# Narrow weight columns loaded from ScalarE's queue; the opening, the convolution block and the end reordered; three fillers per router left out

## The chip, the core and the metric

One core of a Trainium2 chip runs one launch of the whole program. The metric is the device time of that launch in microseconds (us), lower is better.

## The reference

The program is two transformer blocks on one sequence of 256 tokens of width 1024, all in float32. The first has two layers. In each, `x @ w_in` makes inputs of a gated linear attention and of a spatial gating unit; their outputs go through `w_out`, a residual and a layer norm, then through cross attention to 256 memory tokens with another residual and norm, then through 16 experts:

```python
scores = softmax(xt @ w_router + b_router)             # 16 affinities per token
g_sel  = argmax(sum of the top 2 in each of 4 groups)  # one group, two experts in it
y      = sum_e gate[:, e] * ((silu(xt @ w_gate[e]) * (xt @ w_up[e])) @ w_down[e])
x      = layer_norm(alpha * x + y)
```

The second block has an attention of 8 heads beside a state space mixer, whose input `xbc` passes a causal convolution of four taps and a SiLU, then `w_out_a`, `w_out_b`, `w_out`, 16 more experts, and at the end

```python
x = x + sigmoid(x @ w_ple_gate) * (p @ w_ple_proj)
return rms_norm(x, final_norm_g)
```

## The kernel before, in words

**Precision.** A float32 product is made of three products of a faster type: a weight unit (128 x 1024) and each activation are split in a high part and a low part. ScalarE writes the high part (`split`, L1470), VectorE the low part (`split`, L1829) behind it, and TensorE multiplies high by high, high by low and low by high. A dense product of 512 columns takes four units. Six units fit in `w_high`, so ScalarE's `split` of unit n waits until TensorE is done with unit n - 6, and a few splits that stand ahead of a read-out in ScalarE's program tie it to TensorE.

**Engines.** Each engine has its own program, in an order written out by hand, and waits on semaphores. SyncE issues the stream of weight loads, 387 of 1 MB (L595), into nine buffers and, in the expert stages, into other tiles that are free then ("lent"). GpSimd issues the small loads and takes square roots (`root`, L655). PSUM is four slots of two banks. A planner (`plan_job`, `plan_dense`, `between`) hands slots out in the order of TensorE's program; `begin` waits until a slot's last user has freed it.

**The opening.** SyncE loads the two tiles of x (L588), then weights. TensorE transposes both (L912), ScalarE and VectorE split them (L1484, L1849), then the first units, and the product `qk` begins (L749, L750, L754): with `head`, the high products of two units for tile 0, then tile 1, then the low ones. GpSimd waits for two weight loads and then issues six loads of narrow columns (L633): two of the low rank gate, the router, dt, and two of the second router. Each of five of them has 1024 runs of 64 bytes. ScalarE waits for all six (L1628) behind nine splits; VectorE makes the low part (L2201); TensorE then makes `aT` from 16 columns (L931).

**The router** (`router`, `places`, `experts`). Per token tile TensorE transposes, runs fillers (products of constants into an unused bank, L940), multiplies by the router's columns (L954) with one more filler before the fifth of eight, and adds the residual (L1004), with one filler behind it. VectorE ranks and picks; TensorE counts places (L1174, L1176) and gathers each expert's tokens (L996), which ScalarE copies (`packed`, L1539) after it has waited for the gates and written them into `turner` (L1520). In the second block the gates need an `Exp` in between (L1787). Then 16 experts run, each gate, up (L1079) and down (L1114). `FILLERS` (16 in layer 1, two records each) run behind the last expert of a layer while the norm is computed (`norm_of_sums`, `finished`).

**The convolution block.** TensorE makes `xb0`, `xb1`, `xb2`, `z0`, `z1` with attention steps in between (`values_mixed`, `weights_turned` L1334, `scores`). VectorE convolves a block (L2335, L2337). ScalarE reads out, then runs `conv_silu` (L1707, four instructions) of the block before, then `mixed_high` (L1478), whose result VectorE splits and so frees the slot that the next block needs. Behind `z1` `sources` needs all three blocks' SiLU (L1371). Then four gate products follow, each with a scan (`scanned`, L1398 to L1401) and the next scan's decays (`decays`, L1386) behind it.

**The end.** Behind the last expert TensorE multiplies `p` by `w_ple_proj` (`pp`, two units, L799), then transposes x (L912), whose high and low parts it needs for `w_ple_gate` (`pg`, eight units).

The lines that set the order at the router and at the end:

```python
filler(2 * job[name][0] + 1, 1)                   # in router, ahead of the fifth product
filler(2 * job[name][0] + 1, 1)                   # in places, behind the residual
dense_rows(("2.pp0", "2.pp1"), 1, (p_high, p_low))
turn_tiles(x, ("2.x2T0", "2.x2T1"), S["moe_added"])
```

Of the kernel before, what the change touches and what calls it, by code (L numbers as in the profile page):

```python
# [20 lines left out]
ACT = mybir.ActivationFunctionType  # L21
# [3 lines left out]
P = 128  # L25
# [3 lines left out]
SPLIT = 6  # L29
# [4 lines left out]
FILLERS = (8, 16, 0)  # L34
# [17 lines left out]
def build(nc, a, out):  # L52
# [132 lines left out]
    for l in range(DEPTH):  # L185
# [17 lines left out]
        for b, q_slots in enumerate(((s1, s3), (s0, s2))):  # L203
# [15 lines left out]
               "z0": ("oT2", "pT3", "cs"), "z1": ("oT3", "csT", "cb", "xs0", "xs1"), "ga0": ("csb0",), "ga1": ("y0", "csb1"),  # L219
               "gb0": ("y1", "csb2"), "gb1": ("y2", "csb3")}  # L220
# [10 lines left out]
    products, turns_in = slots_of("2.ya0", "2.ya1"), slots_of("2.csb3", "2.y3")  # L231
# [48 lines left out]
    with ExitStack() as ctx:  # L280
# [305 lines left out]
        def _(sp):  # L586
            for t in range(TT):
                sp.dma_start(x[:, t, :], a["x"][0, t * P:t * P + P, :]).then_inc(x_loaded[t], 16)  # L588
            for n, (src, m) in enumerate(stream):
                if raw_behind[n] >= 0:  # L590
                    wait_emptied(sp, raw_behind[n])
# [11 lines left out]
        def _(pool):  # L603
# [22 lines left out]
            with nc.allow_non_contiguous_dma(reason="narrow weight columns, loaded once"):  # L626
                for i in range(2):
                    pool.wait_ge(loaded[i], 16)
                for w, k0, k, dst in ([(a["w_in"][l], O_A, RANK, nar_cols(nar_raw, N_A[l], RANK)) for l in range(DEPTH)]
                                      + [(a["w_router"], 0, NE, router_w[:, :, 0:NE]), (a["w_in_2"][0], O_DT2, SH, nar_cols(nar_raw, N_DT, SH)),  # L630
                                         (a["w_re_2"][0], 0, NE, router_w[:, :, NE:2 * NE]), (a["w_rg_2"][0], 0, 4, router_w[:, :, 2 * NE:2 * NE + 4])]):
                    src = w.rearrange("(c p) n -> p c n", p=P)[:, :, k0:k0 + k]
                    pool.dma_start(dst, src).then_inc(S["narrow_loaded"], 16)  # L633
# [71 lines left out]
        def _(pe):  # L705
# [236 lines left out]
            def router(name, names, m, c0, width, src, normed_before):  # L942

                for t in range(TT):
# [5 lines left out]
                    for c in range(KC):  # L950
                        if c == KC // 2:
                            filler(2 * job[name][0] + 1, 1)
                            pe.wait_ge(S["back_turned"], TT * m + t + 1)
# [212 lines left out]
            def places(name, m):  # L1166

                begin(name)
                filler(2 * job[name][0] + 1, 1)
# [15 lines left out]
            for l in range(DEPTH):  # L1185
                L = f"{l}."

                if l == 0:
                    for t in range(TT):
                        pe.wait_ge(x_loaded[t], 16)  # L1190
                        turn_tiles(x[:, t:t + 1, :], (L + f"xT{t}",))
                else:
# [1335 lines left out]
```

## Time and profile before

| | us |
|---|---|
| median of 3 runs (lowest, highest) | 1446.82 (1443.25, 1447.17) |
| the profiled execution | 1447.49 |
| its span | 1445.8 |
| TensorE busy | 1383.8 (96%) |
| VectorE busy | 596.8 (41%) |
| ScalarE busy | 490.4 (34%) |
| granted TensorE clock, mean | 0.983 |
| DMA, mean over the span | 292 GB/s |

### The profile page before, as it was taken

To read this page: it belongs to the slowest core of one execution; us is meant where nothing else is said; L and a number is where in the kernel's file an instruction comes from. 1 tells how busy PE (TensorE), PEld (TensorE's weight loads), DVE (VectorE), ACT (ScalarE), POOL (GpSimd) and SP (SyncE) were. 2 spreads that over 40 slices of the span, in tenths; PEclk is the share of its full clock that TensorE was granted. 3 is DMA by queue.
4 is the path that set the end of the run, shared out by engine and by line. 5 is a ranking of instruction groups with operands and counts; after the bars stand their busy time and mean duration, and the time that the engine had idled before them with its cause. 6 is when DMAs were issued, how large, how long until landed. Compare 5 with 4: busy or idle time off the path is not lost.

```text
span 1445.8 us, 21087 instructions
## 1 busy us (share of the span) xinstructions
PE 1383.8 (96%) x8985; PEld 1008.7 (70%) x8985; DVE 596.8 (41%) x1004; ACT 490.4 (34%) x692; POOL 55.6 (4%) x95
## 2 busy tenths in 40 slices
PE   5999999999998999999999999899999999999996
PEld 4788977655654788987655554788787776565555
DVE  4586535111114585645211111657766661111125
ACT  4554444111113644443211111466564431111123
POOL 5000000000001000000000000100000000000000
PEclk8999999999999999999999999999998999999998
DMA  9646458999999655628999999753443559999990
GB/s 329 236 147 202 147 199 322 421 420 421 422 420 400 238 171 176 204 87 337 373 420 421 421 420 412 258 174 118 135 157 117 226 235 422 420 421 421 420 373 30
DMA packets 90803, 422.64 MB, mean 292 GB/s; under 512 B 7068, under 2 KB 7232, under 8 KB 53840
## 3 DMA queue, kind: packets, MB, share of 16 engines
q1 hardware_dynamic: 86528, 407.92, 72.2%
q0 software_dynamic: 4176, 13.30, 2.6%
q8 instruction: 74, 1.21, 0.3%
q14 instruction: 25, 0.20, 0.0%
HBM read 420.15 MB, written 1.05 MB: 291 GB/s over the span
## 4 chain that ended last, share of the span: by engine, by line
PE 89%; DVE 4%; ACT 3%; issue 2%; DMA 1%; POOL 1%; SPq 0%; DVEq 0%; POOLq 0%; ACTq 0%
PE ps L1079 23%; PE ps L1114 11%; PE ps L749 5%; PE ps L754 5%; PE ps L750 5%; PE ps L799 4%; PE ps L865 4%; PE ps L804 4%; PE ps L800 4%; PE ps L1126 4%; PE ps L872 4%; PE ps L866 4%; PE ps L996 3%; PE ps L912 1%; PE ps L1093 1%
## 5 line engine op out<-in xcount | busy, mean ns | idle before, releaser
L1829 DVE TENSOR_TENSOR raw_low<-raw,w_high 128x1024 fp32r<-128x1024 f32 x198 | 237.9, 1222 | 167.1 <-ACT w_high L1470 166.5
L1470 ACT ACTIVATE w_high<-raw 128x1024 fp32r<-128x1024 f32 x198 | 206.7, 1057 | 253.6 <-PE ps L754 110.8
L1577 ACT ACTIVATE out_high<-ps,stats 128x512 fp32r<-128x512 f32 x48 | 33.0, 687 | 305.2 <-PE ps L1114 305.2
L749 PE MATMUL ps<-w_high,act_high 128*128 128x512 f32 x272 | 109.8, 404 | 8.4 <-DVE raw_low L1829 3.6
L2154 DVE TENSOR_TENSOR hid<-silu_g,ps 128x256 f32<-128x256 f32 x48 | 29.3, 611 | 210.2 <-PE ps L1079 210.2
L1114 PE MATMUL ps<-raw,hT 128*64 128x512 f32 x488 | 110.3, 592 | 0.0
L750 PE MATMUL ps<-raw_low,act_high 128*128 128x512 f32 x272 | 107.7, 396 | 0.0
L2163 DVE SCALAR_TENSOR_TENSOR out_low<-ps,stats,out_high 128x512 fp32r<-128x512 f32 x48 | 36.1, 752 | 167.6 <-ACT out_high L1577 167.6
L754 PE MATMUL ps<-w_high,act_low 128*128 128x512 f32 x272 | 104.7, 393 | 0.0
L865 PE MATMUL ps<-act_high,w_high 128*128 128x256 f32 x288 | 82.6, 289 | 5.7 <-issue 3.4
L866 PE MATMUL ps<-act_high,raw_low 128*128 128x256 f32 x288 | 82.1, 287 | 0.0
L1079 PE MATMUL ps<-raw,own_odd 128*64 128x256 f32 x704 | 81.5, 381 | 0.0
L872 PE MATMUL ps<-act_low,w_high 128*128 128x256 f32 x288 | 80.2, 287 | 0.0
L799 PE MATMUL ps<-w_high,act_high 128*128 128x512 f32 x192 | 76.3, 398 | 4.0 <-DVE act_low L1849 4.0
L2159 DVE COPY hT<-ps 128x256 f32<-128x256 f32 x45 | 19.1, 425 | 147.4 <-PE ps L1093 147.4
L800 PE MATMUL ps<-raw_low,act_high 128*128 128x512 f32 x192 | 75.7, 394 | 0.0
L1114 PEld LDWEIGHTS ps<-raw,hT 128*64 128x64 f32 x488 | 34.9, 137 | 56.6 <-issue 52.1
L1079 PE MATMUL ps<-raw,own_even 128*64 128x256 f32 x624 | 72.2, 381 | 0.0
L1079 PEld LDWEIGHTS ps<-raw,own_odd 128*64 128x64 f32 x704 | 49.4, 137 | 31.3 <-issue 9.2
L749 PEld LDWEIGHTS ps<-w_high,act_high 128*128 128x128 f32 x272 | 52.2, 192 | 23.1 <-issue 7.8
L655 POOL TENSOR_TENSOR stats<-stats,exponent 128x1 f32<-128x1 f32 (+2 forms) x24 | 21.8, 910 | 1183.8 <-DVE stats L1898 287.1
L1568 ACT ACTIVATE silu_g<-ps 128x256 f32<-128x256 f32 x48 | 18.5, 385 | 139.7 <-PE ps L1079 139.7
(417 smaller groups left out, 2546.2 us busy)
## 6 DMA issues: line engine op xcount, KB each, us to landing
raw<-in_w_down SPq DMA_DIRECT2D x64, 1024.0 KB, 20.4
raw<-in_w_in SPq DMA_DIRECT2D x44, 1024.0 KB, 14.1
raw<-in_w_up SPq DMA_DIRECT2D x43, 1024.0 KB, 15.1
raw<-in_w_gate SPq DMA_DIRECT2D x40, 1024.0 KB, 19.4
work<-in_w_gate SPq DMA_DIRECT2D x26, 1024.0 KB, 16.4
w_lent<-in_w_gate SPq DMA_DIRECT2D x25, 1024.0 KB, 18.9
work<-in_w_up SPq DMA_DIRECT2D x19, 1024.0 KB, 19.2
w_lent<-in_w_up SPq DMA_DIRECT2D x16, 1024.0 KB, 15.0
```

The costliest lines, as they stand in the source:

```text
L749: pe.matmul(bank[:, t, :], xh, wh, start=(k == 0), stop=False)
L750: pe.matmul(bank[:, t, :], xh, wl, start=False, stop=False)
L754: return pe.matmul(bank[:, t, :], src[1][:, k, t * P:t * P + P], weights(n, 512 * c, 512 * c + 512)[0], start=False, stop=(k == KC - 1))
L799: pe.matmul(slot_banks(names[t])[:, b, :], xh, wh, start=(k == 0), stop=False)
L800: pe.matmul(slot_banks(names[t])[:, b, :], xh, wl, start=False, stop=False)
L865: pe.matmul(bank, wh, src[0][:, k, 0:T], start=(k == 0), stop=False)
L866: pe.matmul(bank, wl, src[0][:, k, 0:T], start=False, stop=False)
L872: return pe.matmul(bank, wh, src[1][:, k, 0:T], start=False, stop=(k == KC - 1))
L1079: i = pe.matmul((G, U)[part][OWN * h:OWN * h + OWN, 0:256], own[e // QUAD % 2][:, c, OWN * (e % QUAD):OWN * (e % QUAD) + OWN], w[:, FF * r ...
L1114: i = pe.matmul(y[OWN * h:OWN * h + OWN, :], turned[:, r, OWN * j:OWN * j + OWN], w[:, D * r + 512 * h:D * r + 512 * h + 512], start=(j + ...
L1470: A(split_unit(n)[0], raw_unit(n), ACT.Copy).then_inc(high_ready, 1)
L1829: V.tensor_tensor(split_unit(n)[1], raw_unit(n), split_unit(n)[0].bitcast(F32), ALU.subtract).then_inc(low_ready, 1)
```

## The change

The six narrow loads leave GpSimd's queue for ScalarE's, behind the third unit's split; GpSimd goes on to the small loads of layer 0 at once. The second tile of x is loaded behind the first weights; its transposes go between the high products of the two tiles, and the first two splits go ahead of it. The filler inside each router's products and the one behind the residual go. ScalarE packs before it waits for the gates. At the end of layer 1 a split on VectorE moves behind both scalings, and four more fillers run. The three `conv_silu` move behind `z1`'s splits. The decays go into the middle of the next product, ahead of the scan. At the end, x is transposed before `pp` is made.

```diff
@@ -31,7 +31,7 @@
 TAIL = 3
-FILLERS = (8, 16, 0)
+FILLERS = (8, 20, 0)
 SLOTS = 4
@@ -216,8 +216,8 @@
     between = {"q": ("dtT", "dt"), "v": ("s0",), "xb0": ("pT0", "s1"), "xb1": ("oT0", "pT1", "s2"), "xb2": ("oT1", "pT2", "s3"),
-               "z0": ("oT2", "pT3", "cs"), "z1": ("oT3", "csT", "cb", "xs0", "xs1"), "ga0": ("csb0",), "ga1": ("y0", "csb1"),
-               "gb0": ("y1", "csb2"), "gb1": ("y2", "csb3")}
+               "z0": ("oT2", "pT3", "cs"), "z1": ("oT3", "csT", "cb", "xs0", "xs1"), "ga0": ("csb0",), "ga1": ("csb1", "y0"),
+               "gb0": ("csb2", "y1"), "gb1": ("csb3", "y2")}
     for name, c0 in columns.items():
@@ -228,7 +228,7 @@
     plan_job("2.y3")
-    products, turns_in = slots_of("2.ya0", "2.ya1"), slots_of("2.csb3", "2.y3")
+    products, turns_in = slots_of("2.ya0", "2.ya1"), slots_of("2.y2", "2.y3")
     plan_in(turns_in, "2.uT0", "2.uT1")
@@ -584,9 +584,10 @@
         def _(sp):
-            for t in range(TT):
-                sp.dma_start(x[:, t, :], a["x"][0, t * P:t * P + P, :]).then_inc(x_loaded[t], 16)
+            sp.dma_start(x[:, 0, :], a["x"][0, 0:P, :]).then_inc(x_loaded[0], 16)
             for n, (src, m) in enumerate(stream):
+                if n == 1:
+                    sp.dma_start(x[:, 1, :], a["x"][0, P:2 * P, :]).then_inc(x_loaded[1], 16)
                 if raw_behind[n] >= 0:
@@ -623,14 +624,8 @@
             nc.gpsimd.memset(st[:], 0.0).then_inc(S["consts_ready"], 1)
-            with nc.allow_non_contiguous_dma(reason="narrow weight columns, loaded once"):
-                for i in range(2):
-                    pool.wait_ge(loaded[i], 16)
-                for w, k0, k, dst in ([(a["w_in"][l], O_A, RANK, nar_cols(nar_raw, N_A[l], RANK)) for l in range(DEPTH)]
-                                      + [(a["w_router"], 0, NE, router_w[:, :, 0:NE]), (a["w_in_2"][0], O_DT2, SH, nar_cols(nar_raw, N_DT, SH)),
-                                         (a["w_re_2"][0], 0, NE, router_w[:, :, NE:2 * NE]), (a["w_rg_2"][0], 0, 4, router_w[:, :, 2 * NE:2 * NE + 4])]):
-                    src = w.rearrange("(c p) n -> p c n", p=P)[:, :, k0:k0 + k]
-                    pool.dma_start(dst, src).then_inc(S["narrow_loaded"], 16)
+            for i in range(2):
+                pool.wait_ge(loaded[i], 16)
             def load_small():
@@ -949,7 +944,6 @@
                         if c == KC // 2:
-                            filler(2 * job[name][0] + 1, 1)
                             pe.wait_ge(S["back_turned"], TT * m + t + 1)
@@ -1166,7 +1160,6 @@
                 begin(name)
-                filler(2 * job[name][0] + 1, 1)
                 pe.wait_ge(S["picks_ready"], m + 1)
@@ -1185,14 +1178,9 @@
 
-                if l == 0:
-                    for t in range(TT):
-                        pe.wait_ge(x_loaded[t], 16)
-                        turn_tiles(x[:, t:t + 1, :], (L + f"xT{t}",))
-                else:
-                    turn_tiles(x[:, 0:1, :], (L + "xT0",), S["normed"], TT * (3 * l - 1))
-                second = (lambda: turn_tiles(x[:, 1:2, :], (L + "xT1",), S["normed"], TT * (3 * l - 1) + 1)) if l else None
-                dense_cols(L + "qk", head=(L + "xT0", L + "xT1"), between=second)
+                x_is_in = [(x_loaded[t], 15) if l == 0 else (S["normed"], TT * (3 * l - 1) + t) for t in range(TT)]
+                turn_tiles(x[:, 0:1, :], (L + "xT0",), *x_is_in[0])
+                dense_cols(L + "qk", head=(L + "xT0", L + "xT1"), between=lambda: turn_tiles(x[:, 1:2, :], (L + "xT1",), *x_is_in[1]))
                 if l == 0:
@@ -1427,9 +1415,8 @@
             for k, name in enumerate(("2.ga1", "2.gb0", "2.gb1")):
-                dense_cols(name)
+                dense_cols(name, after_two=lambda: decays(k + 1))
                 scanned(k)
-                decays(k + 1)
             operand_ready(*[f"2.oT{k}" for k in range(AH // 2)])
@@ -1442,8 +1429,8 @@
             operand_ready("2.pT")
+            turn_tiles(x, ("2.x2T0", "2.x2T1"), S["moe_added"])
             dense_rows(("2.pp0", "2.pp1"), 1, (p_high, p_low))
-            turn_tiles(x, ("2.x2T0", "2.x2T1"), S["moe_added"])
             operand_ready("2.x2T0", "2.x2T1")
@@ -1470,6 +1457,15 @@
 
+            def load_narrow():
+
+                with nc.allow_non_contiguous_dma(reason="narrow weight columns, loaded once"):
+                    for w, k0, k, dst in ([(a["w_in"][l], O_A, RANK, nar_cols(nar_raw, N_A[l], RANK)) for l in range(DEPTH)]
+                                          + [(a["w_router"], 0, NE, router_w[:, :, 0:NE]), (a["w_in_2"][0], O_DT2, SH, nar_cols(nar_raw, N_DT, SH)),
+                                             (a["w_re_2"][0], 0, NE, router_w[:, :, NE:2 * NE]), (a["w_rg_2"][0], 0, 4, router_w[:, :, 2 * NE:2 * NE + 4])]):
+                        src = w.rearrange("(c p) n -> p c n", p=P)[:, :, k0:k0 + k]
+                        act.dma_start(dst, src).then_inc(S["narrow_loaded"], 16)
+
             def turned_high(dst, names, width=4):
@@ -1514,13 +1510,16 @@
                     A(turner[:, at_k:at_k + P], ident[:], ACT.Copy, scale=scale)
+                for g in range(GROUPS):
+                    packed(m, 0, g, ps[:, g, :])
+                if m == DEPTH:
+                    act.wait_ge(S["arg_ready"], 1)
+                    A(probs, probs, ACT.Exp).then_inc(S["arg_exp"], 1)
                 act.wait_ge(S["gates_ready"], m + 1)
...
                 i.then_inc(gates_high[m], 1)
-                for g in range(GROUPS):
-                    packed(m, 0, g, ps[:, g, :])
                 act.wait_ge(S["routed"], m + 1)
@@ -1585,11 +1584,12 @@
                 output(NE - 1)
-                split(AHEAD)
+                split(1 if m == DEPTH else AHEAD)
                 if m == DEPTH:
...
                         A(x[:, t, :], flat(ps[:, 2 * s:2 * s + 2, :]), ACT.Copy).then_inc(S["moe_added"], 1)
+                    split(AHEAD - 1)
                 else:
@@ -1620,8 +1620,12 @@
                 if l == 0:
-                    tiles_high(act_high, (L + "xT0", L + "xT1"))
-                split(SPLIT if l == 0 else LATE)
+                    tiles_high(act_high, (L + "xT0",))
+                    split(2)
+                    tiles_high(act_high, (L + "xT1",), 1)
+                    split(1)
+                    load_narrow()
+                split(SPLIT - 3 if l == 0 else LATE)
                 split(3)
@@ -1750,16 +1754,16 @@
                 if b:
-                    conv_silu(b - 1)
                     mixed_high(b - 1)
...
             read_out("2.z0", zs[:, :, 0:512], ACT.Silu)
-            conv_silu(XB_BLOCKS - 1)
             mixed_high(2)
...
             split(4)
+            for b in range(XB_BLOCKS):
+                conv_silu(b)
             read_out("2.z1", zs[:, :, 512:1024], ACT.Silu)
@@ -1783,8 +1787,6 @@
             A(g_prob, g_prob, ACT.Exp).then_inc(S["router_exp"], 1)
-            act.wait_ge(S["arg_ready"], 1)
-            A(probs, probs, ACT.Exp).then_inc(S["arg_exp"], 1)
             experts(DEPTH)
@@ -1898,7 +1900,8 @@
                 scaled(0)
-                split(1)
+                if before_last is None:
+                    split(1)
                 nonlocal means
@@ -2119,6 +2122,7 @@
                     mix_scaled(1)
+                    split(1)
                     input_low("2.xT")
@@ -2193,8 +2197,9 @@
                     V.memset(aT, 1.0)
+                    split(AHEAD)
                     tiles_low(act_low, act_high, (L + "xT0", L + "xT1"))
-                    split(SPLIT)
+                    split(SPLIT - AHEAD)
                 split(3)
```

## Rows read from the trace of the kernel before

**Rows 1.** Part 1 of the page: busy time of each engine

```profile
PE 1383.8 (96%) x8985; PEld 1008.7 (70%) x8985; DVE 596.8 (41%) x1004; ACT 490.4 (34%) x692; POOL 55.6 (4%) x95
```

**Rows 2.** The waits of PE over the whole span: in total, times, longest

```profile
PE ps L931 <- DVE nar_low L2201: 5.7, 1, 5.7
...
PE ps L799 <- DVE act_low L1849: 4.0, 1, 4.0
PE ps L749 <- DVE raw_low L1829: 3.6, 1, 3.6
PE ps L865 <- issue: 3.4, 1, 3.4
PE ps L912 <- DVE work L1947: 3.3, 1, 3.3
...
PE ps L1334 <- DVE work L2362: 2.1, 1, 2.1
...
PE ps L1079 <- ACT own_even L1539: 1.5, 1, 1.5
```

**Rows 3.** The chain, 12 to 31 us: start, us, what; the last narrow load

```profile
22.30 6.52 DMA router_w<-in_w_rg
```

**Rows 4.** SyncE weight loads issued before 30 us: ns min/median/max

```profile
L595 SPq DMA_DIRECT2D raw<-in_w_in x10: 426/2144/6220, 1.7 to 20.6; - x10
```

**Rows 5.** Timeline of ScalarE behind block xb1: start, us, engine, line

```profile
987.83 1.28 ACT L1707 ACT_TABLE_LOAD   x1
989.12 1.70 ACT L1707 ACTIVATE xbc<-xbc,colc 128x256 f32<-128x256 f32 x4
```

**Rows 6.** Timeline behind block z1, all engines

```profile
1035.26 1.06 ACT L1470 ACTIVATE w_high<-raw 128x1024 fp32r<-128x1024 f32 x1 [1.66 <-PE ps L754]
...
1036.13 0.60 PE L1371 MATMUL ps<-xbc 128*128 128x256 f32 x2
```

**Rows 7.** Stretches: length, PE, PEld, DVE, ACT, POOL busy, clock, DMA share, GB/s

```profile
912.50:919.30 6.80, 5.83 (x22) 5.19 (x22) 4.53 (x5) 1.71 (x3) 1.88 (x3) 0.50 1.05 384
991.00:997.80 6.80, 6.15 (x29) 6.18 (x30) 6.54 (x18) 4.53 (x12) 0.00 (x0) 0.50 0.00 0
1083.20:1090.00 6.80, 6.80 (x17) 4.90 (x16) 2.69 (x8) 2.44 (x3) 0.00 (x0) 0.50 0.07 30
1103.70:1107.00 3.30, 3.30 (x9) 2.60 (x8) 1.76 (x6) 1.48 (x1) 0.00 (x0) 0.50 0.00 0
1410.90:1417.60 6.70, 4.78 (x11) 3.80 (x12) 6.70 (x7) 3.78 (x4) 0.00 (x0) 0.50 0.02 4
1146.80:1148.70 1.90, 1.90 (x13) 1.72 (x14) 1.90 (x2) 0.81 (x1) 0.00 (x0) 1.00 0.61 78
```

**Rows 8.** Timeline of PE behind block gb0

```profile
1081.89 2.57 PE L1386 MATMUL ps<-work,ident 16*128 16x256 f32 x8
```

**Rows 9.** The chain in the last router, 1164 to 1200 us

```profile
1177.94 0.52 PE ps L940 x2
...
1182.80 0.43 PE ps L940 x2
```

**Rows 10.** Timeline at the end of layer 1, PE and DVE

```profile
903.02 7.17 PE L940 MATMUL ps<-tri,ident 128*128 128x256 f32 x32
...
907.80 1.22 DVE L1829 TENSOR_TENSOR raw_low<-raw,w_high 128x1024 fp32r<-128x1024 f32 x1
```

**Rows 11.** DMA issues of 1367.8 to 1369.9 us: KB each, us to landing

```profile
raw<-in_w_down SPq DMA_DIRECT2D x1, 1024.0 KB, 27.6
```

**Rows 12.** Timeline of the end, 1367 us on

```profile
1367.87 2.13 SPq L595 DMA_DIRECT2D raw<-in_w_down  x1
...
1396.23 1.94 PE L1114 MATMUL ps<-raw,hT_last 128*64 128x512 f32 x8
...
1406.94 1.91 PE L912 MATMUL ps<-ident,x_res 128*128 128x128 f32 x16
1408.01 1.94 ACT L1484 ACTIVATE act_high<-ps 128x1024 fp32r<-128x1024 f32 x2 [4.44 <-PE ps L912]
```

## The prediction

> **What bounds the kernel now.** I read the page's first part: TensorE is busy for 1383.8 of 1445.8 us [rows 1], so time can come from two places only, its idle time and the products that it makes at the low clock. The waits of PE give the idle time by what ended it, and eight or so single waits carry it: 5.7 us for the narrow columns, 4.0 at the end of the kernel, 3.6 in the opening, 3.4 and 2.1 in the convolution block, 3.3 at the end of layer 1, 1.5 ahead of the last experts [rows 2]. The stretches give the clock: it stood at 0.50 for 6.8, 6.8, 6.8, 3.3 and 6.7 us at five places with work waiting [rows 7]. Three of them begin behind one of those waits; the two from 1083.20 and 1103.70 follow no wait, but a run of scans (64 columns) and decays (16 rows) [rows 8]. A wait thus costs itself and, where the clock falls behind it, half of what PE does in the slow stretch. The sum below is against the profiled execution's own 1447.49 us; the median of the runs is 0.67 lower, and the difference is carried over to it.
>
> **The end of the kernel.** PE makes `pp` up to 1406.94, then 16 transposes in 1.91 us, then waits 4.0 us while ScalarE (1.94 us for two tiles) and VectorE split them [rows 2, 12]. With the transposes first, the same splits run beside `pp`, which lasts 5.7 us. I follow it: ScalarE copies x by about 1402.2, the transposes end at 1403.3, `pp`'s second unit, now split behind the copies, is ready at 1404.5, one product of 2.8 us after the first, `pp` ends at 1408.9, and VectorE has the second low part at about the same time. So 3.8 of the 4.0 us go. The clock then has no reason to fall: of the 4.78 us that PE worked at 0.50 half comes back, 2.4. **Minus 6.2.** The cover is `pp` itself; VectorE is nearly late, by estimate within 0.5 us.
>
> **The end of layer 1.** The split that leaves VectorE's way to the last scaling is one of 1.22 us [rows 10], and PE's wait of 3.3 us ends with that scaling [rows 2]. 1.2 us. Sixteen fillers took 7.17 us [rows 10], so four more take 1.8 and fill what was idle; 0.3 us of idle time is left, the clock stays, and of 5.83 us worked at 0.50 half comes back, 2.9. **Minus 4.1.** The moved split is needed only when the next product begins, over 2 us later.
>
> **Scans and decays.** The work is the same. A decay run was 8 records in 2.57 us, partly at the low clock [rows 8], right behind 2.7 us of scan. Now they stand 5 us apart, with full products between. The same pair at 1063 and the scan alone at 1110 did not lower the clock, so one of the two alone should not. Half of 6.8 and 3.3 [rows 7]: **minus 5.0**. Bounds 0 and 5.0. New waits: the first decays now need the slot of `pT`, free at about 1058.0 when PE comes at 1058.1 (an estimate from the order of VectorE's instructions); I take 0, at most 1.
>
> **The convolution block.** Before, `mixed_high` stood behind a table load of 1.28 us and four SiLU in 1.70 us [rows 5], and PE waited 3.4 us for the slot that it leads to [rows 2]. 2.9 of them go. With them goes the stretch at 0.50 from 991.00, in which PE worked 6.15 us: 3.1. VectorE gets its softmax block earlier, so that most of the wait of 2.1 us at L1334 goes too: 1.9. Together 7.9. Against it: all twelve SiLU now stand behind the split that ended at 1036.3 with `z1` done, and PE wanted them at 1036.13 [rows 6]. Nothing is left to do meanwhile; `z1` is not even read out. 3 x 1.70 = 5.1 us of idle time that was not there, and it is as long as those behind which the clock fell. I take 1.5 for that, between 0 and the 3.4 that the longest slow stretch cost. 7.9 - 5.1 - 1.5: **minus 1.3**, with a range from -3 to +3. By the Trainium skill (ScalarE: Activation LUTs, "Rules for kernel authors") activations of one table set are to be grouped, and a load costs about 2.7 us. The trace has it at 1.28 us, and here it counts only where PE waits behind ScalarE. By the skill's figure four loads fewer would be 10.8 us and the part a clear gain; this is an estimate from that page, and the sum does without it.
>
> **The routers.** A filler was 0.52 us ahead of the fifth product and 0.43 behind the residual [rows 9]. The first two lie on the path, as VectorE's half of the copy is done by then; part of the first is given back, since the second tile's transposes wait for VectorE's scaling (0.4 is left, 0.25 in the last router). The third is on the path in the last router alone: in the others VectorE's picks come at the same time, and move up with the router. So 0.9, 0.9 and 1.1 us, **minus 2.9**; bounds 1.4 (one filler each) and 4.4 (all three). The residual itself, 3.5 us of full products, keeps the clock.
>
> **Gates behind packing.** In layers 0 and 1 no wait stood there, so 0; the gates come some 2 us later and have 0.8 us of slack left before the next gather. In the last block 1.5 us of waiting goes [rows 2], and about 0.5 comes back when the second gather waits for VectorE. But the experts run on DMA: the last tile but one was issued at 1367.87 and landed 27.6 us later, at 1395.5, and PE used it at 1396.23 [rows 11, 12]. The load that starts this stream waits for the tokens' low parts and doesn't move with ScalarE's order. So PE can gain no more than these 0.8 us. **Minus 0.3.** The routers' gain stays, as it moves those low parts too.
>
> **The opening.** ScalarE now splits the second tile only after the transposes that PE makes behind its first products. PE's wait of 3.6 us [rows 2] gets 1.7 shorter, but PE waits 1.1 for the second tile and the third unit is ready at the same time as before. ScalarE comes to the narrow loads at about 17 us instead of GpSimd at 11.9. Then six units must be split, six times 1.22 us on VectorE [rows 10], and the narrow ones. With c for one issue, `aT` starts at about 26.1 + 6 c; it started at 30.1, behind a last load issued at 22.30 and 6.52 us on its way [rows 3]. SyncE's issues took between 0.426 and 6.22 us, 2.144 in the middle, the long ones when its queue was full [rows 4]. A narrow load has twice the runs of a dense one (1024 to 512) but 1/16 of its bytes. I take 0.43 for the first two and 0.8 for the others: 4 us, `aT` at 30.1, **0**. Bounds: c = 0.43 gives -1.4; c = 2.144 gives +9; c = 6.22 gives +33. I take the low end because the trace's long issues belong to transfers of 1 MB, which take 2.5 us each at the measured rate. GpSimd's loads come 11 us earlier and compete with weights that have room; x's second tile comes one load later and is not waited for. Both 0.
>
> **The sum.** 6.2 + 4.1 + 5.0 + 1.3 + 2.9 + 0.3 + 0 = 19.8 us. 1447.49 - 19.8 = 1427.7 for a profiled execution, 1427.0 for the median.
>
> **The rivals.**
> - *The clock falls all the same.* Of the sum, 10.3 us are clock (2.4, 2.9, 5.0). If the slow stretches only move, as they begin behind low activity of any kind, half to all of that is lost: 1432 to 1437. For it: the transposes, 16-column products and short idle times stay. Against it: the stretches at 1063 and 1110 above. 0.17.
> - *Transposes keep the clock low.* They are much of what PE does at the end of layer 1. If they didn't count, 2.9 us there stay lost: 1430. Against it: transposes and the products behind them ran at 1.00 from 1146.80 on, behind a wait of 1.8 us [rows 7]. 0.06. The Trainium skill (TensorE: Matmul & The Clock Gate, "Part 4: PE-mode transpose") says that a transpose does not count as busy in the same way; the trace speaks against it for these.
> - *The SiLU wait costs all.* Clock and wait at their upper bounds, and the block loses 4 instead of gaining 1.3: 1432. 0.08.
> - *DMA sets the experts' pace.* If the streams don't move up with the routers, 2.9 us are lost: 1430. For it: 0.8 us of margin. Against it: the load that opens each stream waits for the same VectorE work. 0.08.
> - *ScalarE is held by the narrow loads.* If each issue blocks as SyncE's longest did, 6.22 us, ScalarE stands still for 37 us, every split behind it too, and `aT` starts 33 us late: 1460, slower than before. It decides from c = 3.7 us on, where the whole sum is used up. For it: ScalarE's queue is in order and 5120 short runs go through it. 0.09, of which 0.04 lies between, within 0.3%.
> - *More than the sum.* The opening gains its 1.4 and all fillers count: 1424. Inside the forecast.
>
> **How the numbers follow.** The forecast case (1422 to 1431) has 0.52. The predicted time is 1427. The range reaches over the clock's case and the SiLU's: 1420 to 1438. 0.3% (4.3 us) is about what a measurement of this kernel can tell. Faster by more: 0.52 + 0.17 + 0.06 + 0.08 + 0.08 = 0.91, less 0.02 for several of them together, 0.89. Within: 0.04 + 0.02 = 0.06. Slower: 0.05.
>
> **What would show it.** Right: no wait over 1 us at L799 at the end and no 0.50 there; a wait under 0.5 us ahead of L912 at the end of layer 1; no stretch at 0.50 in the gate products; a new wait of 5 us at L1371; SyncE unchanged; six issues on ScalarE near 17 us that take some 4 us in all; the wait at L931 about 4 us. Wrong: ScalarE idle or issuing for over 10 us in the opening; a wait at L1079 or L1114 for DMA; slow stretches at new places.

## The result, and the profile after

The changed kernel takes 1459.23 us (median of 4 runs, 1457.79 to 1461.09) against 1446.92 us before: the ratio is 1.0092, with a 95% interval of 1.0072 to 1.0112. It is 12.3 us slower; 1427 had been forecast, 20 us faster. The profiled execution's span is 1458.1 us, against 1445.8.

Part 1 of the page of the changed kernel, and the lines of its DMA part that count packets by queue:

```profile
PE 1377.3 (94%) x8975; PEld 1000.6 (69%) x8975; DVE 596.0 (41%) x1004; ACT 484.7 (33%) x688; POOL 50.3 (3%) x89
...
DMA packets 96852, 422.66 MB, mean 290 GB/s; under 512 B 13212, under 2 KB 13360, under 8 KB 59888
## 3 DMA queue, kind: packets, MB, share of 16 engines
q1 hardware_dynamic: 86528, 407.92, 71.6%
q0 software_dynamic: 3984, 12.96, 2.5%
...
q10 hardware_dynamic: 6240, 0.34, 0.3%
```

The same lines of the kernel before:

```profile
DMA packets 90803, 422.64 MB, mean 292 GB/s; under 512 B 7068, under 2 KB 7232, under 8 KB 53840
## 3 DMA queue, kind: packets, MB, share of 16 engines
q1 hardware_dynamic: 86528, 407.92, 72.2%
q0 software_dynamic: 4176, 13.30, 2.6%
```

TensorE is busy for 6.5 us less than in [rows 1] and its idle time grew by 18.8. The narrow loads show as a queue of their own, q10: 0.34 MB in 6240 packets. GpSimd's queue, q0, lost the same 0.34 MB and only 192 packets.

The waits of PE in the changed kernel; the first column after the colon is the total, then the number of times, then the longest:

```profile
PE ps L744 <- DVE raw_low L1831: 27.1, 2, 23.7
PE ps L1359 <- ACT xbc L1711: 5.0, 1, 5.0
...
PE ps L1073 <- issue: 3.5, 1, 3.5
...
PE ps L926 <- DVE nar_low L2206: 1.8, 1, 1.8
...
PE ps L794 <- ACT gate_b L1490: 1.1, 1, 1.1
```

Against [rows 2] the waits of 3.4 us (third block), 3.3 us (end of layer 1), 2.1 us (L1334) and 4.0 us (end) are gone. In their place stand one of 23.7 us in the opening, one of 5.0 us for the twelve SiLU, and 3.5 us in the last experts that no semaphore explains.

The time by stage is had by subtracting the starts of the same PE instruction in the timelines of the two kernels. Each difference below is from one such start to the next:

| stage (start before, after) | forecast | measured |
|---|---|---|
| opening, to the first router's products (230.55, 251.38) | 0 | +20.8 |
| router of layer 0, to its gather (243.28, 263.41) | -0.9 | -0.7 |
| to aT of layer 1 (477.17, 498.57) | 0 | +1.3 |
| router of layer 1 (676.64, 697.99 to 689.38, 709.92) | -0.9 | -0.8 |
| end of layer 1 (903.02, 923.53 to 920.89, 937.38) | -4.1 | -4.0 |
| convolution block, to L1334 behind z0 (1022.76, 1031.07) | -7.9 | -8.2 |
| the same, behind z0, to ga0's decays (1050.21, 1068.10) | +6.6 | +9.6 |
| gate products and scans, to the next transposes (1118.71, 1133.54) | -5.0 | -3.1 |
| last router, to its gather (1185.53, 1199.50) | -1.1 | -0.9 |
| packing and first expert, to L1103 (1195.76, 1214.41) | -0.3 | +4.7 |
| the end, from the last addition (1395.10, 1413.77) to the span's end | -6.2 | -6.4 |

The rows add up to +12.3. Three are off by more than 2 us: the opening, the part behind z0, and the first expert. Each row compares one execution of each kernel. What the low clock costs at one place differs between executions (see the last section), so 1 to 3 us in a single row say little by themselves.

### The profile page after: what moved, and what is told of

Its sections match the earlier page's. It is cut to its first block, busy times and chain, and to the rows that moved or that the text cites. A ratio compares the mean times of both kernels' runs of the same rounds, so it can differ in the third digit from the quotient of the medians.

```text
span 1458.1 us, 21065 instructions
## 1 busy us (share of the span) xinstructions
PE 1377.3 (94%) x8975; PEld 1000.6 (69%) x8975; DVE 596.0 (41%) x1004; ACT 484.7 (33%) x688; POOL 50.3 (3%) x89
## 3 DMA queue, kind: packets, MB, share of 16 engines
q10 hardware_dynamic: 6240, 0.34, 0.3%
## 4 chain that ended last, share of the span: by engine, by line
PE 88%; DVE 4%; ACT 3%; ACTq 2%; issue 2%; POOL 0%; DMA 0%; DVEq 0%; POOLq 0%
PE ps L1073 23%; PE ps L1108 11%; PE ps L744 5%; PE ps L745 5%; PE ps L749 5%; PE ps L1120 4%; PE ps L860 3%; PE ps L794 3%; PE ps L795 3%; PE ps L799 3%; PE ps L867 3%; PE ps L861 3%; PE ps L990 3%; ACTq L1467 2%; PE ps L907 2%
## 5 line engine op out<-in xcount | busy, mean ns | idle before, releaser
L744 PE MATMUL ps<-w_high,act_high 128*128 128x512 f32 x272 | 110.9, 408 | 34.4 <-DVE raw_low L1831 27.1
L794 PE MATMUL ps<-w_high,act_high 128*128 128x512 f32 x192 | 75.2, 392 | 0.0
```

What stands on the lines that cost most here:

```text
L744: pe.matmul(bank[:, t, :], xh, wh, start=(k == 0), stop=False)
L794: pe.matmul(slot_banks(names[t])[:, b, :], xh, wh, start=(k == 0), stop=False)
```

## The experiments

Each is a kernel of its own. All times are medians, except where one run is named. The ratio is against runs of the kernel before on the same chip, whose medians were 1445.3 to 1446.4 us. The experiments ran on three chips, so a difference between two of them carries the error of both ratios.

### Where the opening's 21 us come from

Timeline of the changed kernel, the issues on ScalarE's queue and the first activation behind them:

```profile
15.51 1.06 ACTq L1467 DMA_DIRECT2D work<-in_w_in  x2
...
16.59 14.26 ACTq L1467 DMA_DIRECT2D router_w<-in_w_router  x1
...
30.88 6.08 ACTq L1467 DMA_DIRECT2D work<-in_w_in  x1
36.99 4.40 ACTq L1467 DMA_DIRECT2D router_w<-in_w_re  x1
41.41 3.14 ACTq L1467 DMA_DIRECT2D router_w<-in_w_rg  x1
44.59 1.06 ACT L1457 ACTIVATE w_high<-raw 128x1024 fp32r<-128x1024 f32 x1 [27.12 <-issue]
```

ScalarE computes nothing for 27.1 us: its own program is held at the issues. The first two took 0.43 and 0.60 us, the third 14.3 us. DMA packets by queue from 20 to 24 us, while SyncE's weights (q1), GpSimd's small loads (q0) and the narrow loads (q10) all run:

```profile
q0 software_dynamic: 267, 0.90, 62.5%
q1 hardware_dynamic: 270, 0.52, 37.7%
q10 hardware_dynamic: 269, 0.02, 5.1%
```

The same from 36 to 40 us, when GpSimd's loads are done:

```profile
q1 hardware_dynamic: 698, 1.39, 96.5%
q10 hardware_dynamic: 699, 0.04, 14.0%
```

The counts are equal, though a packet was 3.4 KB on average in q0, 2 KB in q1 and 64 bytes in q10: the DMA engines serve the queues one packet each in turn, and a packet of 64 bytes costs a turn as a large one does. The Trainium skill (DMA: Bandwidth & Descriptors, "Queues, rings and completion order") has the same rule, each engine round-robins between its queues a packet at a time; the trace agrees. The Trainium skill's sentence that the SyncE and ScalarE path is generally faster (the same page, "Issuing engine by pattern") does not hold for these loads.

**Narrow loads back on GpSimd.**

```diff
-                    load_narrow()
...
+                for w, k0, k, dst in ([(a["w_in"][l], O_A, RANK, nar_cols(nar_raw, N_A[l], RANK)) for l in range(DEPTH)]
...
+                    pool.dma_start(dst, src).then_inc(S["narrow_loaded"], 16)
             def load_small():
```

> The changed kernel with the six narrow loads back on GpSimd's queue, ahead of its small loads; all else as changed. Theory 1 (ScalarE's queue makes a packet of every 64-byte run: the page after counts 6240 packets for 0.34 MB on a queue of its own, and GpSimd's queue lost only 192): aT starts at 29 to 31 us instead of 53.2, ScalarE has no issue over 2 us, the page has about 90,800 packets, and the time falls by 20 to 23 us, to 1437 to 1439. Rival (the opening's new order of transposes and splits is what is late, whatever the queue): aT stays later than 40 us and the time over 1448.

Measured: 1439.46 us (1435.7 to 1443.77), ratio 0.9944 (0.9920 to 0.9969). aT starts at 29.96 us. Its page's packets, and its wait for aT:

```profile
DMA packets 90804, 422.66 MB, mean 294 GB/s; under 512 B 7068, under 2 KB 7232, under 8 KB 53840
...
q0 software_dynamic: 4176, 13.30, 2.7%
```

```profile
PE ps L932 <- DVE nar_low L2202: 4.4, 1, 4.4
```

Moving the loads to ScalarE's queue cost 19.8 us: that is the queue and, with it, GpSimd's small loads, which had come ahead. With both undone the change is 7 us faster than before. The new order of transposes and splits is neither better nor worse up to here: aT starts 0.1 us earlier than before. GpSimd, too, was held once, for 5.7 us before its fourth issue, but no engine waited for it:

```profile
13.88 0.89 POOL L634 DMA_DIRECT2D router_w<-in_w_router  x1
20.47 0.89 POOL L634 DMA_DIRECT2D work<-in_w_in  x1 [5.70 <-issue]
```

**GpSimd's loads held back.**

```diff
+            pool.wait_ge(S["narrow_loaded"], 16 * (DEPTH + 4))
             def load_small():
```

> The changed kernel, but GpSimd issues its small loads only once all six narrow loads have landed; the narrow loads stay on ScalarE. Theory 1 (an issue on ScalarE waits until its queue has room for 1040 more packets, and the DMA engines serve the queues one packet each in turn, so that GpSimd's 4 KB packets slow the narrow ones from about 185 to 65 per us): the third issue takes 6 to 9 us instead of 14.3, ScalarE is free again at 34 to 40 us instead of 44.6, the time falls by 4 to 10 us, to about 1452. Rival (writing 1024 short descriptors costs ScalarE's queue its 3 to 14 us by itself): the issues stay at 14.3, 6.1, 4.4 and 3.1 us and the time at 1459 or above.

Measured: 1449.19 us (one run, so it has no interval). aT starts at 42.93 us, 10.3 us earlier than in the changed kernel. Its issues on ScalarE, and its packets from 20 to 24 us:

```profile
15.17 1.08 ACTq L1468 DMA_DIRECT2D work<-in_w_in  x2
...
16.28 5.71 ACTq L1468 DMA_DIRECT2D router_w<-in_w_router  x1
22.02 5.85 ACTq L1468 DMA_DIRECT2D work<-in_w_in  x1
27.90 4.05 ACTq L1468 DMA_DIRECT2D router_w<-in_w_re  x1
31.98 2.29 ACTq L1468 DMA_DIRECT2D router_w<-in_w_rg  x1
```

```profile
q1 hardware_dynamic: 693, 1.39, 96.6%
q10 hardware_dynamic: 692, 0.04, 14.3%
```

The third issue fell from 14.26 to 5.71 us with the same descriptors, so writing them does not take a fixed time of its own. The pace of the narrow packets rose from 67 to 173 per us. In the changed kernel 871 packets had been served when the third issue was through, of 3120 issued by then (three of 1040), so some 2250 were outstanding. The reading is that an issue waits for room in its queue. The size of that room is not shown: 2520 and 2780 packets were outstanding behind the fourth and fifth issue, and 2600 behind the third issue here. Ten of the 21 us came from moving GpSimd's small loads ahead, where they take every third turn; aT's start says so as well as the one time.

**The order of the narrow loads** (on the best version so far, below).

```diff
-[(a["w_router"], 0, NE, ...), (a["w_in_2"][0], O_DT2, SH, ...), ...]   # one semaphore, narrow_loaded
+[(a["w_in_2"][0], O_DT2, SH, ..., "narrow_loaded"), (a["w_router"], 0, NE, ..., "router_loaded"), ...]
-                    act.wait_ge(S["narrow_loaded"], 16 * (DEPTH + 4))
+                    act.wait_ge(S["narrow_loaded"], 16 * (DEPTH + 1))
+                if m == 0:
+                    pe.wait_ge(S["router_loaded"], 48)
```

> The padded kernel (narrow loads on GpSimd's queue, SiLU between the blocks, padding) with the narrow loads in another order: those of the low rank gate and of dt first, on the semaphore that ScalarE waits for, and the three of the routers behind them on one of their own, for which only the first router waits. Theory 1 (aT waits 4.4 us only because ScalarE waits for all six loads, of which the last lands at 28.8 us, and the clock falls behind that wait): the wait at L932 falls under 1 us, aT starts at 25.7 to 27 us, the stretch at 0.50 from 28.6 us may go, and the time falls by 4 to 8 us, to 1422 to 1426. Rival (all loads of the opening share one pace, so that the units come later by as much): PE waits for a unit or its low part instead, and the gain is under 2 us.

Measured: 1421.17 us (1420.1 to 1424.87), ratio 0.9826 (0.9796 to 0.9856), 8.4 us less than the version it starts from. In the two traces the difference is 4.0: the opening gives 6.5, and slow stretches at other places take 2.5 back. The wait is 0.39 us, and aT starts at 25.11:

```profile
25.11 0.28 PE L934 MATMUL ps<-act_high,nar_high 128*16 128x256 f32 x1 [0.39 <-DVE nar_low L2209]
```

No stretch at 0.50 is left in the opening. One wait took the place of the old one, 1.1 us for `b_a`. GpSimd issues it behind all six narrow loads, as before; PE now comes earlier.

### The convolution block

Timeline of the changed kernel where PE comes out of z1's product:

```profile
1046.11 4.88 ACT L1711 ACTIVATE xbc<-xbc,colc 128x256 f32<-128x256 f32 x12
...
1051.13 1.19 PE L1359 MATMUL ps<-xbc 128*128 128x256 f32 x2 [4.96 <-ACT xbc L1711]
```

The wait is the 5 us that were forecast. Behind it the clock fell. The columns are length, PE, PEld, VectorE, ScalarE and GpSimd busy with counts, granted clock, DMA share, GB/s; the second row is the first expert, the third stands for the gate products:

```profile
1050.10:1056.90 6.80, 5.76 (x23) 5.44 (x24) 1.86 (x3) 2.06 (x5) 0.00 (x0) 0.50 0.00 0
1207.10:1213.90 6.80, 5.43 (x24) 3.15 (x25) 0.43 (x2) 0.59 (x2) 0.00 (x0) 0.50 1.01 419
1091.00:1098.00 7.00, 7.00 (x32) 5.32 (x31) 4.04 (x4) 3.19 (x4) 0.00 (x0) 1.00 0.45 152
```

**SiLU between the blocks.**

```diff
                     mixed_high(b - 1)
                 copied(b)
+                if b:
+                    conv_silu(b - 1)
...
             copied(3)
+            conv_silu(XB_BLOCKS - 1)
             split(4)
-            for b in range(XB_BLOCKS):
-                conv_silu(b)
```

> The changed kernel, but each block's four SiLU stand right behind mixed_high and the copy behind it, and the third block's ahead of z1's splits, instead of all twelve behind these splits. Theory 1 (PE waits 5.0 us at L1359 for twelve SiLU, and the clock falls behind that wait): the wait at L1359 goes, the slow stretch from 1050 us goes with it, the waits of 3.4 and 2.1 us of the kernel before stay away, and the time falls by 6 to 8.5 us, to 1451 to 1453. Rival (the SiLU have no free place: wherever they stand on ScalarE they push the read-outs, and PE waits for slots): waits of 1.3 to 3.4 us come back in the blocks before, and the gain is under 3 us.

Measured: 1451.62 us (1449.32 to 1454.41), ratio 1.0048 (1.0028 to 1.0069): 7.6 us less than the changed kernel. The wait at L1359 is gone, the stretch from 1050 us too, and the waits of 3.4 and 2.1 us stayed away. A shorter stretch at 0.50, from 1033.0 to 1036.4 us, is there instead, just behind the wait at z1. PE's second wait at z1, 1.35 us for the read-out of z0, is still there. Before, PE waited 2.1 us at L1334 just ahead of it and came only when the read-out was done.

**Scans and decays as before.**

```diff
-                dense_cols(name, after_two=lambda: decays(k + 1))
+                dense_cols(name)
                 scanned(k)
+                decays(k + 1)
```

The plan of slots goes back with it.

> The changed kernel with the scans and decays as before: each scan behind its gate product, and the decays behind the scan. Theory 1 (a run of scan and decays lowers the clock, as at 1083 and 1103 us of the kernel before): one or two stretches at 0.50 come back behind gb0 and gb1, and the time rises by 3 to 5 us, to 1462 to 1464. Rival (the slow stretches are a matter of when the run meets the chip's own period, not of its length): no stretch there, or as many elsewhere, and the time within 1.5 us of 1459.2.

Measured: 1465.22 us (1464.15 to 1468.58), ratio 1.0134 (1.0112 to 1.0155), 6.0 us more than the changed kernel, and above what either theory gave. Of the rise only 2.1 us lie in the gate products: one slow stretch came back there, and behind `gb0` as in [rows 7]:

```profile
1102.90:1109.70 6.80, 6.80 (x17) 4.88 (x16) 2.69 (x8) 2.68 (x3) 0.00 (x0) 0.50 0.04 16
```

The rest of the trace's 5.7 us is a slow stretch at 219 us, in code that is the same in both (1.6), and 2.0 us at the first expert, where the unexplained stall was 5.9 us long instead of 3.5. So the separation is worth 2 to 3 us by these traces, not 5. In the changed kernel 1.1 us of it is given back: PE is early at `ya` and waits for `gb1`'s read-out (the wait at L794 above).

### The first expert

**Gates before packing.**

```diff
-                for g in range(GROUPS):
-                    packed(m, 0, g, ps[:, g, :])
                 if m == DEPTH:
...
                 i.then_inc(gates_high[m], 1)
+                for g in range(GROUPS):
+                    packed(m, 0, g, ps[:, g, :])
```

> The changed kernel with ScalarE's order at the experts put back: it waits for the gates and writes them, then packs. Theory 1 (with the packing first PE enters the experts' code 1.6 us earlier, and the instructions of it are not there yet: 3.5 us at L1073 in which it waits for nothing that the profile shows): the stall goes, a wait of 1.5 us for packing comes back, no stretch at 0.50 begins near 1207 us, and the time falls by 3 to 5 us, to about 1455. Rival (the stall belongs to where the code lies or to that one execution, not to ScalarE's order): the stall stays beside the wait for packing, and the time is 1459 to 1461.

Measured: 1457.97 us (1455.36 to 1459.81), ratio 1.0077 (1.0052 to 1.0102). Theory 1 had the slow stretch right and the stall wrong. No stretch at 0.50 begins near 1207 us, but only 1 us of the stall went, and the time is 1.3 us less, not 3 to 5. The wait for packing came back and most of the stall stayed:

```profile
PE ps L1073 <- issue: 2.5, 1, 2.5
...
PE ps L1073 <- ACT own_even L1538: 1.5, 1, 1.5
```

PE went on at 1208.65 us, against 1208.47 in the changed kernel. So what it lacks comes at its own time, and ScalarE's order only decides how PE spends the time until then. The DMA queues of the changed kernel from 1206 to 1208.5 us:

```profile
q1 hardware_dynamic: 141, 1.03, 99.2%
q8 instruction: 1, 0.02, 2.4%
```

Each of the traces with the stall shows such an instruction packet, of 16384 bytes, that begins 3.3 to 5.1 us behind the end of PE's branch into the experts; PE always stops behind 12 products and goes on 1.2 to 1.5 us after the packet has ended. The longest stall, 5.9 us, stands where it came latest. The kernel before has this packet too, from 1192.67 to 1193.62 us, and no stall: its 32 products ran without a break from 1191.11 to 1194.78 us, where the changed kernel stopped behind 12.

**Padding that is never executed**, on a kernel with two parts put right (narrow loads on GpSimd, SiLU between the blocks). First that kernel without the padding:

> The changed kernel with two parts put right: the six narrow loads on GpSimd's queue, and the SiLU between the blocks, behind mixed_high and the copy. Theory 1 (the two losses are apart in time and add up): 1459.2 less the 19.8 and the 7.6 that the two runs alone gave, 1431 to 1433. Rival (part of each was clock that only moved, and moves again): 1435 or more, with slow stretches at places that were at full clock in either run.

Measured: 1432.79 us (1429.43 to 1434.25), ratio 0.9907 (0.9891 to 0.9924), 26.4 us less than the changed kernel. The two gains, 19.8 and 7.6, add up to within 1 us. The chain of waits at its first expert:

```profile
1173.44 1.52 PE ps L1079 x12
1174.96 4.30 issue
1179.26 3.76 PE ps L1079 x20
```

Then with 16 fillers at the end of the branch that is not taken:

```diff
                 with nc.body(f"all_{m}", valid_engines=[mybir.EngineType.PE]):
                     experts_all(m)
+                    if m == DEPTH:
+                        filler(0, 16)
                     pe.br(f"met_{m}")
```

> The kernel of the run before (narrow loads on GpSimd's queue, SiLU between the blocks) with 16 fillers added at the end of the branch of the last experts that is not taken, so that nothing more is executed but the code behind it lies elsewhere. Theory 1 (where the taken branch starts within a piece of code that is loaded whole decides how many of PE's instructions are there at first: 12 products in the changed kernel, over 32 in the kernel before): the stall of 4.4 us at L1079 goes wholly or by more than half, and the time falls by 3 to 6 us, to 1426 to 1429. Rival (the second piece is asked for a fixed time behind the branch and PE comes 1.5 us too early): the stall stays at 3.5 to 4.5 us and the time within 1 us.

Measured: 1429.56 us (1425.66 to 1430.6), ratio 0.9878 (0.9859 to 0.9897), 3.2 us less, in the traces 3.5. The intervals of the two ratios overlap a little; the trace shows the cause. The stall is gone:

```profile
1177.81 1.22 PE ps L998 x8
1179.03 0.26 PE ps L1105 x2
1179.30 4.89 PE ps L1081 x43
```

Nothing that runs was changed, only where the code of the taken branch lies. So the stall hangs on the place of the code, and with the packet above it reads as code that is not there yet. The Trainium skill (Advanced Engine Details and Errata, "ISA Cache") says that instructions are held in lines of 16 KB, 256 instructions; the packet of 16384 bytes has the size of one such line. That the 64 instructions of padding moved the edge of a line past the first products is the likely reading; where the edges lie no trace shows. Of the 5.1 us that PE is earlier at the first expert against the unpadded kernel, 1.6 are lost again at the last three down products before the last addition. There PE now waits for weights, 0.9 us in all, which the unpadded kernel did not do at these products:

```profile
PE ps L1116 <- DMA gate_a<-in_w_down: 0.5, 1, 0.5
...
PE ps L1116 <- DMA raw<-in_w_down: 0.2, 1, 0.2
PE ps L1116 <- DMA gate_b<-in_w_down: 0.2, 1, 0.2
```

**The routers' fillers put back** (into the changed kernel).

```diff
                         if c == KC // 2:
+                            filler(2 * job[name][0] + 1, 1)
...
                 begin(name)
+                filler(2 * job[name][0] + 1, 1)
                 pe.wait_ge(S["picks_ready"], m + 1)
```

> The changed kernel with the three fillers of each router put back. Theory 1 (they lie on PE's path): the routers take 0.9, 0.8 and 0.9 us more, 2.6 together, and the time is 1461 to 1463 if the stall at the last experts stays; 36 instructions of PE more ahead of the branch may move that stall, and if it goes, 1456 to 1458. Rival (they kept the clock high or filled time in which PE would wait): the routers take less than 1 us more in all.

Measured: 1457.94 us (1456.17 to 1461.24), ratio 1.0086 (1.0064 to 1.0108). The three routers take 0.9, 0.8 and 0.9 us more, as forecast. The 36 PE instructions also moved the code, and the stall is gone: the 32 products of the first expert run in one piece from 1204.99 us. The two nearly cancel in the total. Leaving the fillers out gained 2.4 us and, by this reading, lost about as much again through the place of the code.

**Gates before packing, padded.**

> The padded kernel with ScalarE's order at the experts put back (gates, then packing). Theory 1 (in the last experts the loads set the pace once PE comes more than 0.8 us earlier, so packing first is worth little): a wait of 1.5 us for packing comes back at the first expert, the waits for DMA at the last experts' down products go, and the time rises by 0 to 1 us. Rival (the packing is worth what PE's wait was): it rises by 1.5 us or more.

Measured: 1429.42 us (1428.1 to 1430.05), ratio 0.9878 (0.9844 to 0.9911), the same as without the swap. The wait of 1.5 us for packing is back, the waits for weights are 0.6 and 0.2 us, not gone. In the traces PE loses 1.7 us at the first expert by the swap and has 1.0 of them back by the last addition. That leaves 0.7 for packing first, too little for the times to tell.

### The end

**The end as before.**

```diff
+            dense_rows(("2.pp0", "2.pp1"), 1, (p_high, p_low))
             turn_tiles(x, ("2.x2T0", "2.x2T1"), S["moe_added"])
-            dense_rows(("2.pp0", "2.pp1"), 1, (p_high, p_low))
```

> The changed kernel with the end as before: the two units of pp first, then x transposed. Theory 1 (the end was worth 6.4 us, 3.8 of waiting and the rest clock): the wait of 4.0 us ahead of the first product of pg comes back, a stretch at 0.50 behind it, and the time rises by 5.5 to 7 us, to 1465 to 1466. Rival (the wait went, but the clock's part came from where the run happened to be): 3.8 to 4.5 us, 1463 to 1464.

Measured: 1466.66 us (1462.62 to 1469.89), ratio 1.0145 (1.0110 to 1.0181), 7.4 us more than the changed kernel. The four times spread over 7.3 us, so the medians alone don't separate the two theories (about 6 us or 4). The traces do: from the last addition to the end this one takes 51.6 us, the changed kernel's 44.3. The wait is back, and behind it a stretch at 0.50 from 1426.5 to 1433.3 us:

```profile
PE ps L794 <- DVE act_low L1851: 4.0, 1, 4.0
```

## Why the prediction was wrong

**The opening** was the step that failed: "I take 0.43 for the first two and 0.8 for the others: 4 us, `aT` at 30.1, **0**." It alone accounts for 20.8 of the 32 us by which the forecast was off. The form of the step was right. aT at 26.1 + 6 c, with the six measured issues (0.43, 0.60, 14.26, 6.08, 4.40 and 3.14 us, 28.9 together), gives 55.0 us, and it started at 53.2. The size of c was wrong, 4.8 us on average instead of 0.67. I argued that SyncE's long issues belonged to transfers of 1 MB. A narrow load carries a sixteenth of those bytes, and one was held for 14.3 us. What counted was packets: 1040 for each of them, served at the pace of the other queues' packets. The rival "ScalarE is held by the narrow loads" named this mechanism, and had 0.09. That its time of 1460 was met is luck: it has `aT` 33 us late, which was 23.1 late, and the rest came from the other rows of the table. Its point of decision, c = 3.7, is 4.0 by the prediction's own formula (26.1 + 6 c = 30.1 + 19.8). [Rows 4] had an average of 4.8 within its bound of 6.22, not the single issue of 14.26. What also went unseen is that GpSimd's loads, 11 us earlier, compete with the narrow ones. I had weighed them against the weights only.

**Packing before the gates** (-0.3 forecast, +4.7 measured). The waits were read rightly: 1.6 us were gained up to the first product. The loss is the stall of 3.5 us and the slow clock behind it, 2.7 (half of the 5.43 us worked at 0.50). The stall is no matter of this edit: undoing it left most of the stall, and padding or 36 more instructions took it away. Without the stall, packing first was worth 0.7 us, and the forecast's reason why it is not 1.5, that the last experts wait for weights, held.

**Behind z0** (+6.6 forecast, +9.6 measured). The wait for SiLU was 5.0 us as forecast (5.1). The clock cost 2.9 instead of 1.5, within the bound of 3.4. Not seen was the wait of 1.35 us for z0's read-out, which the wait at L1334 had covered. The two waits ahead of z0 went as forecast, and 8.2 us with them. The block as a whole lost 1.4 us instead of gaining 1.3. The rival for it has a loss of 4 at the upper bounds, but 7.9 - 5.1 - 3.4 is a loss of 0.6.

**Scans and decays** (-5.0 forecast, -3.1 measured). The slow stretches went, but 1.1 us came back as the wait for `gb1`. Put back, the order cost 2.1 us and brought one of the two stretches back, not both.

**Right** were the end of layer 1, the routers, and the end of the kernel. The end gained 6.4 us by the table, and 7.3 us by the trace with it undone; the routers 2.4 and 2.6. The end of layer 1 was read from the table alone, where the wait of 3.3 us fell to 0.4 and the slow stretch went. With it falls the rival that transposes keep the clock low there.

**The clock** also fell at new places: from 483.4 us, with the same waits as before, it cost 1.3 us. The rival that the slow stretches only move is thus true in part. It counted 10.3 us of the sum as clock and left out the 3.1 of the convolution block, which makes 13.4.

The best version that was run has the change's reordering with the narrow loads on GpSimd, those that are needed first in front, the SiLU between the blocks and the padding. It takes 1421.2 us, 1.7% less than the kernel before.

## What to carry to other kernels

Cost a DMA issue by its packets. On ScalarE's queue each run of 64 bytes was a packet and took the turn of a large one, and the engine that issued the loads stood still until most of them were served. Such loads belong on an engine whose program can wait, here GpSimd, and what is needed first should have a semaphore of its own. A wait in which the profile names no releaser, just behind a branch, may be code loading. Padding the branch that is not taken is a test of it that executes nothing more.

## What the runs showed that was not expected

- GpSimd's queue moved the narrow columns in 192 packets where ScalarE's took 6240, for the same 0.34 MB. By the sizes in the two traces, 80 packets of 4096 bytes on GpSimd's queue stand for 5120 of 64 bytes on ScalarE's.
- Where the code of a taken branch lies was worth 3.2 us here, and 36 instructions more, spread over the program ahead of it, were enough to take the stall away.
- Slow stretches of the clock came and went without a change in the work. The padded kernel with the gates first ran at 0.50 from 197.4 to 200.8 us, the padded kernel at 1.00, though the two are the same up to there. The opening of layer 1, with waits of 1.3 and 1.2 us ahead of it in every trace, ran at 0.50 for 3.4 us in the changed kernel. With all of it 21 us earlier it ran at 1.00 in the padded kernel, and at 0.50 again in the one with the gates first. By 650 us that one was 3.8 us behind. Single terms of 1 to 3 us in one trace are within that.
